# Storing a tile's result in twenty transfers of 7, 7, 7, 7 and 4 partitions instead of four of 32

## The reference, cut to what matters

```
scores = einsum('thpd,hpkd->thpk', q, sub_keys);  s_top, i_top = top_k(scores, 16)
best, sel = top_k(all 256 sums of a pair of tops, 16);  idx = the chosen experts;  gate = softmax(best)
u_e = expert_down[idx];  v_e = expert_up[idx]
act = gelu(einsum('thkd,td->thk', u_e, xb))
x = x + gate2 * einsum('thkd over k', gate * act, v_e)
return rms_norm(x, g_final)
```

## Time and profile before

| what | us |
|---|---|
| median of 3 runs | 2823.51 |
| profiled execution, its own time | 2821.43 |
| its span, first to last instruction | 2819.6 |
| DMA busy share over the span | 99% in nearly every fortieth |
| chain that ended last: DMA | 57% of the span |
| VectorE busy | 1898.9 (67%) |
| TensorE busy | 1934.2 (69%) |
| GpSimd busy | 1121.5 (40%) |

### The profile page before, as it was taken

The page is one execution under the profiler, slowest core; times in us unless marked ns, Lnnn a source line. Parts: engine busy times, 40 slices in busy tenths (PEclk is TensorE's granted clock), DMA queues, the critical chain, the costliest instruction groups (busy, mean ns, idle before and its releaser), DMA issues.

```text
span 2819.6 us, 38636 instructions
## 1 busy us (share of the span) xinstructions
PE 1934.2 (69%) x13316; PEld 891.0 (32%) x13316; DVE 1898.9 (67%) x4714; ACT 1211.2 (43%) x3867; POOL 1121.5 (40%) x1030
## 2 busy tenths in 40 slices
PE   5898898788886666675656766666666656665553
PEld 4555354354342222231312222232222323221110
DVE  5687676785755867576667757677676756676554
ACT  1346445554443434454434434444343444444333
POOL 0144344344433444444444444443444444344332
PEclk9998898899887676656666566665767667565555
DMA  9899999999999999999999999999999999999997
GB/s 405 347 381 421 393 420 412 409 421 417 421 418 398 421 421 421 421 421 421 418 421 419 418 421 417 421 417 420 417 421 419 412 422 413 420 415 421 421 420 295
DMA packets 168645, 1160.02 MB, mean 411 GB/s; under 512 B 18945, under 2 KB 25601, under 8 KB 35202
## 3 DMA queue, kind: packets, MB, share of 16 engines
q0 software_dynamic: 147456, 1073.81, 92.2%
q1 hardware_dynamic: 20994, 83.75, 7.5%
HBM read 1149.61 MB, written 7.86 MB: 411 GB/s over the span
## 4 chain that ended last, share of the span: by engine, by line
DMA 57%; PE 22%; DVE 11%; ACT 6%; issue 3%; another core or an unknown queue 0%; POOL 0%; SPq 0%; DVEq 0%; POOLq 0%; ACTq 0%
DMA work<-experts,expert_rows 43%; DMA more_ring<-experts,expert_rows 9%; PE ps_sum L912 7%; PE ps_small L878 5%; DMA weights<-experts,expert_rows 4%; DVE work L1572 4%; PE ps_m L828 4%; PE ps_m L772 2%; PE ps_m L783 1%; ACT diag L1149 1%; ACT weight L1144 1%; PE ps_m L792 1%; PE ps_wide L854 1%; ACT act_out L1142 1%; DVE more_ring L1572 1%
## 5 line engine op out<-in xcount | busy, mean ns | idle before, releaser
L663 POOL DMA_INDIRECT work<-experts,expert_rows x818 | 898.1, 1098 | 1363.7 <-PE ps_sum L912 1214.0
L1572 DVE CUSTOM_DVE_ANT_0 work<-work 128x1024 f32<-128x1024 f32 x818 | 999.5, 1223 | 611.8 <-DMA work<-experts,expert_rows 601.1
L912 PE MATMUL ps_sum<-work,diag 128*32 128x256 f32 x6544 | 719.7, 524 | 666.4 <-ACT diag L1149 647.4
L1142 ACT ACTIVATE act_out<-act_in 128x1 f32<-128x1 f32 x1024 | 207.4, 203 | 1183.3 <-DVE act_in L1572 1165.6
L912 PEld LDWEIGHTS ps_sum<-work,diag 128*32 128x32 f32 x6544 | 149.9, 126 | 1135.1 <-ACT diag L1149 1046.0
L1149 ACT ACTIVATE diag<-const,weight 128x32 f32<-128x32 f32 x1024 | 329.1, 321 | 33.5
L1144 ACT ACTIVATE weight<-gate,act_out 128x1 f32<-128x1 f32 x1024 | 301.7, 295 | 33.3
L878 PE MATMUL ps_small<-h_t,weights 128*128 128x128 f32 x1408 | 305.7, 384 | 1.9 <-ACT wide L1128 1.1
L878 PEld LDWEIGHTS ps_small<-h_t,weights 128*128 128x128 f32 x1408 | 261.6, 278 | 135.5 <-issue 129.8
L1572 DVE CUSTOM_DVE_ANT_0 more_ring<-more_ring,work 128x1024 f32<-128x1024 f32 x122 | 149.2, 1223 | 96.3 <-DMA more_ring<-experts,expert_rows 92.7
L663 POOL DMA_INDIRECT more_ring<-experts,expert_rows x122 | 134.7, 1104 | 182.9 <-PE ps_sum L912 179.1
(11 more groups left out here) (200 smaller groups left out, 1909.2 us busy)
## 6 DMA issues: line engine op xcount, KB each, us to landing
work<-w_ada SPq DMA_DIRECT2D x12, 2048.0 KB, 23.3
work<-sides SPq DMA_DIRECT2D x24, 576.0 KB, 7.5
work<-experts,expert_rows POOLq DMA_INDIRECT x818
weights<-sides SPq DMA_DIRECT2D x16, 576.0 KB, 25.2
weights<-w_in SPq DMA_DIRECT2D x3, 2048.0 KB, 16.9
more_sides<-sides SPq DMA_DIRECT2D x10, 576.0 KB
x_buf<-x SPq DMA_DIRECT2D x8, 512.0 KB
weights<-w_out SPq DMA_DIRECT2D x2, 2048.0 KB, 36.2
```

Source lines behind the costliest of these rows:

```text
L663: nc.gpsimd.indirect_dma_start(ring[x.ring], None, experts, bass.IndirectOffsetOnAxis(ap=rows_flat[:, x.column:x.column + 1], axis=0),).th ...
L912: last = nc.tensor.matmul(ps_sum[quarter(c), x.group, :], diag[:, x.ring, :], ring[x.ring][:, D + c * QCOLS:D + (c + 1) * QCOLS], start=x. ...
L1142: nc.scalar.activation(act_out[:, s:s + 1], act_in[:, s:s + 1], ACT.Gelu).then_inc(s_gelu, 1)
L1572: nc.vector.tensor_tensor_reduce(down, down, h2_spread[x.segment % 2], 1.0, 0.0, ALU.mult, ALU.add, act_in[:, x.g % TURN:x.g % TURN + 1]). ...
```

## The change: what it does

For tiles 0 to 6 each of the four DMAs of `store_out` becomes five, of partitions 0 to 6, 7 to 13, 14 to 20, 21 to 27 and 28 to 31 of the quarter. The bytes and their places in `out` are the same. Each of the 20 DMAs adds 16 to `s_out`, so the counts waited for become 320 a tile (`STORED`) in place of 64. The last tile, stored in two halves, keeps one DMA for a quarter.

```
+STORE_ROWS, LAST_ROWS = (0, 7, 14, 21, 28, 32), (0, QROWS)
+STORED = 16 * QUADS * (len(STORE_ROWS) - 1)
...
                 if t >= 2:
-                    sp.wait_ge(s_out, 64 * (t - 1))
+                    sp.wait_ge(s_out, STORED * (t - 1))
...
             def store_out(n):
                 t, first, end = ENDS[n]
                 sp.wait_ge(s_final, n + 1)
+                rows = LAST_ROWS if t == TILES - 1 else STORE_ROWS
                 for c in range(QUADS):
-                    sp.dma_start(out_v[t, c][:, first:end, :], y[quarter(c), first:end, :]).then_inc(s_out, 16)
+                    for lo, hi in zip(rows[:-1], rows[1:]):
+                        sp.dma_start(out_v[t, c][lo:hi, first:end, :],
+                                     y[c * QROWS + lo:c * QROWS + hi, first:end, :]).then_inc(s_out, 16)
...
-            sp.wait_ge(s_out, 64 * (TILES + 1))
+            sp.wait_ge(s_out, STORED * (TILES - 1) + 2 * 16 * QUADS)
...
                 if t >= KEPT_FROM:
-                    dve.wait_ge(s_out, 64 * (t - 1))
+                    dve.wait_ge(s_out, STORED * (t - 1))
...
-                    dve.wait_ge(s_out, 64 * t)
+                    dve.wait_ge(s_out, STORED * t)
```

## The result

| kernel | median us | runs | lowest to highest |
|---|---|---|---|
| before | 2824.01 | 4 | 2822.45 to 2825.38 |
| after | 2841.69 | 4 | 2838.61 to 2843.43 |

The ratio is 1.0057, its 95% interval 1.0045 to 1.0069. On 2824 us that is +16.1 us (+12.7 to +19.5): the change made the kernel slower, by about what the prediction had worked out for the loaded engines alone. The medians themselves lie 17.7 us apart; the ratio's interval holds both figures. The forecast of 2824.5 us was wrong, and its range of 2812.5 to 2832 too. The profiled execution took 2841.19 us, its span 2839.4.

The account below looks back on a forecast made before the run. The prediction took the work of one slow DMA engine as the bound; 2821.43 us profiled + 1 for the uneven deal, the waits at nothing, gave 2822.4, or 2824.5 us against the median, range 2812.5 to 2832.

Parts of the forecast that it names:

- The bound: Whole kernel: compute engines wait for gathers, and the time is the work of one slow DMA engine, 11.2 us behind the middle.
- The price and the deal: Stores of tiles 0 to 6: 46.7 ns a piece; four engines get +16.1 us, three +10.5, nine -10.5.
- The fixed choice of engines: Stores: each DMA's engines always begin at the same one, so four engines get 20 of a tile's 128 rows.
- What of it reaches the end: End of kernel: 16.1 less the 11.2 us lead gives +4.9 at most, -10.5 at least; taken as +1 us.
- rival B: No slack: slowest engine among the loaded, each tile longer by 2.3 or 1.5 us; +14 taken, 2837.5 us; chance 0.12.
- the sign that the prediction gave for B: Profile after: even tile lengths, with all seven tiles 2.3 us longer.
- The slack of the others: Engines other than the slow one: the middle one's lead of 11.2 us at the end, only a floor of the slack.
- Rival A: Relief pays: the slow engine and its follower get no pieces; -9 us (-6 to -10.5), 2814.5 us; chance 0.30.
- The waits: VectorE's reads behind the longer stores: six waits of some 6 to 7 us, costed at nothing, 42 us without cover.
- Rival C: The waits show: part of the 42 us comes through, +10 to +42, +20 taken, 2843.5 us; chance 0.06.
- The end: Last windows: DMA share falls earlier and in steps, the last gather ending on several engines instead of one.

Follow-up runs that it names:

- e5: Kernel before plus fourteen extra DMAs a tile (tiles 0 to 6) of 1 partition x 4 KB to a scratch tensor: 2821.04 beside 2821.28 us, ratio 1.0000.
- e6: Kernel before plus fourteen extra 4 KB-row DMAs a tile (tiles 0 to 6) of 2 partitions, 96 and 97: 2831.03 beside 2821.28 us, ratio 1.0038.
- e10: Kernel before plus twenty-eight extra DMAs a tile (tiles 0 to 6) of 1 partition x 4 KB: 2823.92 beside 2820.17 us, ratio 1.0016.
- e2: Kernel before, with the residual loads of tiles 3 to 6 held back on SyncE until just ahead of their reader: 2824.34 beside 2824.48 us, ratio 1.0002.
- e8: Kernel before plus fourteen extra DMAs a tile (tiles 0 to 6) of 4 partitions x 4 KB: 2838.86 beside 2821.28 us, ratio 1.0063.
- e9: Kernel before plus fourteen extra DMAs a tile (tiles 0 to 6) of 3 partitions x 4 KB: 2832.41 beside 2820.17 us, ratio 1.0045.
- e11: Kernel before plus twenty-eight extra DMAs a tile (tiles 0 to 6) of 2 partitions x 4 KB: 2847.55, ratio 1.0097.
- e4: Kernel before plus fourteen extra DMAs a tile (tiles 0 to 6) of 2 partitions x 4 KB, 0 and 1: 2838.39 beside 2824.48 us, ratio 1.0039.
- e1: Kernel before with a tile's result stored by sixteen DMAs of 32 partitions x one 1 KB piece: 2825.45 beside 2824.48 us, ratio 0.9998.

## Why the prediction was wrong, point by point

**The bound: right.** One engine sets the end, before and after; what is put on others up to their slack is free (e5: 15.6 us for nothing). One reading is loose: a 9 in the row of DMA digits says 90% or more, not 99%; that the share is near 100% is shown by the windows with 1.01 and 1.02.

**The price and the deal: right.** 46.7 ns a piece, taken from one window, gives 10.5 us for 8 rows (measured +10.7) and 16.1 us with the completions for 7 (measured +16.1). With intervals of 3.4 to 4 us either way, so close a fit is in part luck. So is the price itself: the 501 packets of that window are not all pieces of 1 KB: 23 are of 4 KB and some are completions of 4 B, and the two kinds nearly make up for each other. In the trace the 1 KB pieces of tile 2's store took 46 ns each (median). The fixed choice of engines holds (e6). The Trainium skill, "DMA: Bandwidth & Descriptors", section on why a DMA increments its semaphore by 16, lets a plain DMA run on the largest number up to 16 that divides the slowest dimension of both sides that isn't of size 1, here the rows: the completions of 7, 4, 3, 2, 8 and 30 rows (7, 4, 3, 2, 8 and 15) agree. A DMA of one row is another matter: its count of rows is 1, and its next dimension has 1024 elements, which 16 divides. The one completion of each in e5 says that it runs on one engine, and the measurement decides.

**The failed step** is "What of it reaches the end". The prediction put the loaded engine's lead at 11.2 us, "the upper bound if the slow engine isn't a loaded one", and took +1. The condition was false: the slowest engine is one of the four loaded ones (by the runs of two chips together the fourth of the order in which rows are dealt), and so is its follower, the second. The step from 4.9 down to 1, four fifths taken away, had no row for its size either. A slow engine has no slack, so the toll is paid whole, 48 pieces a tile, in every tile: rival B's mechanism, at the upper of its two prices, and the sign that the prediction gave for B, even tile lengths about 2.3 us longer, is what came. It had 0.12, though the prediction itself counted 7 engines of 16 for it. What was held against this, that a choice by row count has nothing to do with who is slow, was no evidence: it is the very reason for taking 7 in 16.

**The slack of the others** was mis-sized too. The middle engine's 11.2 us at the end was called a floor, rightly: the first engine had 26.7 us (e10). The prediction's reason, that an engine ahead by the gathers under way idles for lack of requests, so that the end shows only the last such lead, fits this, but no run shows it by itself. By e10 the 16.1 us would have been free on engines like the first.

**Rival A** (relief) fell with the same condition. The Trainium skill, same page, section on latency and other measured facts, says that engines 7 and 15 are usually slower than the rest. With the deal on the lowest-numbered engines, as the same page has it, the two stragglers here would be the fourth and the second of 16; the trace names no engine, so which of the two statements fails here is open.

**The waits: right that they cost nothing, their sizes about right.** Forecast were six waits of 6 to 7 us; five came, of 4.7 to 7.3 us, 27.2 us in all, at no cost (e2 with 23.9 us). The six are tiles 2 to 7, but tile 7 has no load. The 22.3 us more for store and load behind it were too many: in tile 4 the two took 38.8 us from the first issue to the landing (1231.59 to 1241.29 + 29.1) for 20.2 before, 18.6 more. The load for tile 2 was forecast at 595.4 and issued at 595.94, but that is luck: 4.05 of its 22.8 us are the later start of the first store, and 18.8 the longer store. "With no hole in the DMA share" was wrong: there is a dent to 0.94, in e2 as well, and it costs nothing since the engine that matters stays busy. Rival C had no part.

**The end: wrong.** "The last gather ending on several engines" did not come, as the slowest engine was pushed back with the others.

**What stays open:** why these two engines are slow; whether the slowest is the fourth on every chip; why leaving the store out gave 8.2 us where 10.5 were due (within the interval). And the places rest on four steps, +0, +11, +12.7 and +17.8, the last three with intervals of about 4 us either way and from three chips; only together with the ends of the runs do they name the engine.

No version that stores every tile beats the kernel before. With the slow engine at the fourth place, each DMA that runs on at least four engines puts work on it, and 32 rows, two for each of 16 engines, is already the even deal.

## What to carry to other kernels

Where DMA is the bound, ask which engine ends last and what share of a transfer falls on it: in these runs the row count of a plain DMA (its largest divisor up to 16) decides how many engines share it, always from the same first one. A mean share near 100% and equal bytes say nothing of that. And when an estimate hangs on who the slow engine is and no row shows it, the sides should get the chances that counting gives, or a run with a few rows should find it out first.

## What the runs showed of the hardware

- One engine sets the pace of a stream that 16 share: one of the first four in the order of the deal (the toll of 16.1 us, interval 12.7 to 19.5), the fourth if e8 and e9 are put together. The second is about 4 us ahead of it in 2800 (3.8 by e11, 4.6 by e4), and the first has 26.7 us of slack (e10).
- Work on the first engine is free up to 26.7 us, on the slowest it is paid in full: a small store of 3.7 MB in all, dealt 20 rows of 128 to the slow engine instead of 8, costs 0.57% of the kernel.
- Twelve more DMAs a tile, each with 16 completions, 1344 small packets in all, cost nothing (e1, 0.9989 to 1.0007).
- Waits of up to 7.1 us of VectorE, on which the freeing of buffers hangs, with 7.9 gathers under way, dent the DMA share to 0.96 and cost nothing (e2, 0.9993 to 1.0011).
